# The residual of four layer norms: from a TensorE product with a scaled identity to a ScalarE write into the accumulator banks

## The chip, the cores and the metric

The kernel runs on one core of one Trainium2 chip. The metric is device time in microseconds (us) of one execution. Three runs of the kernel before took 918.62, 918.8 and 917.6 us; their median is 918.62 us.

## The reference

Two blocks follow each other on an activation `x` of 256 rows by 1024 columns. The first block has two sub-layers with an RMS norm after each (`x = x + rms_norm(m)`); nothing in it changes here. The second block has two layers, and each layer has a mixer and a feed-forward network (FFN), so four sub-layers:

```
ALPHA = (2.0 * DEPTH) ** 0.25
for layer in range(2):
    mix = concatenate([o_main, o_mem]) @ w_out      # layer 0: NSA attention, layer 1: MoBA attention
    x = layer_norm(ALPHA * x + mix, ln1_g[layer], ln1_b[layer])
    ffn = conv_ffn(x, ...)                          # up, convolution, gelu gate, down (2816 -> 1024)
    x = layer_norm(ALPHA * x + ffn, ln2_g[layer], ln2_b[layer])
```

The change touches how `ALPHA * x` gets into the sum with `mix` or `ffn`. Each of the four layer norms reads that sum from PSUM.

## The kernel before, in words

The 256 rows are two row blocks `q` of 128 rows. The output of a sub-layer for block `q` is 128 x 1024 and lies in two PSUM banks, `2q` and `2q+1` (index `z` is the half of 512 columns), so all four banks 0 to 3 hold the output of a sub-layer. Banks 4 and 5 take attention logits, 6 the transposed probabilities, 7 the attention outputs; in the FFN banks 4 to 7 take the up products.

Matrix products with weights are split: ScalarE (ACT) rounds a weight unit of 128 x 1024 from `raw` to `whi` (L622, called "split" or "hi" below), VectorE (DVE) computes the rest `wlo` (L628, "lo"), and TensorE (PE) adds three rounded products, activation high times weight high, low times high, high times low (L681, L684 and L687 in `pe_chunk`; L778 in `pe_project`, six instructions of 512 columns per unit and row block). The units arrive by DMA through four `raw` buffers and six split buffers.

The order of the work is written out by hand. `EVEN`, `ODD`, `NSA` and `MOBA` are lists of steps, `feed(l)` builds the list of FFN `l`. Each engine walks through the same list and does its own part of every step, strictly in that order. A step `("log", g)` is: PE computes logits (L858), DVE adds the mask and takes the minimum (L971), ACT takes the exponentials (L984). `("mul", g)` is DVE's normalisation, `("turn", g, side)` the transposes (L867) and a copy by ACT (side 0, L1031) or DVE (side 1, L1039), `("val", g)` the value product, `("fin", g)` the output's split, `("proj", s, n, q)` one unit of the output projection, and `("chunk"/"tile")` an input projection. With every step that uses a weight unit, ACT first splits units up to four ahead. `("cmp",)` is the logits of NSA's compressed keys (L1803 on PE, L1928 to L1933 on DVE, L1866 on ACT). `("T", k, q)` transposes a finished `x` (L716), ACT copies it as the high part `thi` (L723), DVE computes the low part `tlo` (L730). `("norm", ...)` is the layer norm: DVE's statistics (L1146), two passes into `rows` and `x` (L1152, L1160), and for `q` = 1 one weight "lo" (L628) between these two passes.

The residual is a step `("add_x", s, q)`, `pe_add_x`: two products of the matrix `scaled` (the identity times ALPHA, made by POOL at the start) with `x[:, q, half z]`, both in plain fp32, with `start=True` into banks `2q` and `2q+1`:

```
p.fill(2 * q + z, (*normed, q, z))
p.i.matmul(ps[:, 2 * q + z, :], scaled[:, :], x[:, q, half[z]], start=True, stop=False)
```

There are eight such steps: two in each of `NSA`, `feed(0)`, `MOBA`, `feed(1)`. In a mixer they stand in the middle of the list; banks 0 and 1 (NSA) or 0 to 2 (MoBA) were until then the banks that the input projections used in turn ("turn banks"). In an FFN `add_x 0` is the first step and `add_x 1` comes right after the transposes `T` of block 1. The projection `("proj", s, 0, q)` and the first `down` step accumulate onto what is there. `p.fill` waits until the bank's previous content has been read.

Of the kernel before, what the change touches and what calls it, by code (L numbers as in the profile page):

```python
# [263 lines left out]
def _build(nc, ctx, inp, out_dram, plan):  # L264
# [15 lines left out]
    tb = sb("tb", [P, 12 * T])  # L280
    stat = sb("stat", [P, 1024])
    ident = sb("ident", [P, P])
    scaled = sb("scaled", [P, P])
    tri = sb("tri", [P, T])
    relb = sb("relb", [32, 12])
    cols = sb("cols", [P, 4])
# [245 lines left out]
    for g in nsa[2:]:  # L532
# [9 lines left out]
        ("tile", "a_q", 2), ("log", n0), ("turn", m0, 0), ("turn", m0, 1), ("tile", "a_q", 3), ("mul", n0), ("turn", m1, 0),  # L542
        ("comp", 1), ("comp", 2), ("val", m0), ("turn", m1, 1), ("fin", m0), ("log", n1), ("tile", "a_q", 4), ("turn", n0, 0),
        ("turn", n0, 1), ("comp", 3), ("log", n2), ("tile", "a_q", 5), ("mul", n1), ("val", m1), ("mul", n2), ("fin", m1),
        ("turn", n1, 0), ("turn", n1, 1), ("log", n3), ("cmp",), ("add_x", "a", 0), ("turn", n2, 0), ("proj", "a", 0, 0),
        ("add_x", "a", 1), ("cmp2",), ("log", n4), ("cmpt", 0), ("turn", n2, 1), ("proj", "a", 1, 0), ("log", n5), ("mul", n3),
        ("proj", "a", 0, 1), ("val", n0), ("turn", n3, 0), ("mul", n4), ("proj", "a", 1, 1), ("fin", n0), ("turn", n3, 1), ("cmpt", 1),
        ("proj", "a", 2, 0), ("val", n1), ("fin", n1), ("turn", n4, 0), ("val", n2), ("fin", n2), ("log", n6), ("turn", n4, 1),
        ("proj", "a", 2, 1), ("mul", n5), ("val", n3), ("turn", n5, 0), ("fin", n3), ("log", n7), ("mul", n6), ("proj", "a", 3, 0),
# [19 lines left out]
        ("tile", "b_k", 3), ("turn", g2, 0), ("turn", g2, 1), ("tile", "b_q", 3), ("mul", g3), ("val", g2), ("fin", g2),  # L569
        ("turn", g3, 0), ("log", g4), ("turn", g3, 1), ("mul", g4), ("tile", "b_k", 4), ("chunk", "b_v1", 0, 0), ("val", g3),  # L570
        ("chunk", "b_v1", 0, 1), ("fin", g3), ("chunk", "b_v1", 1, 0), ("chunk", "b_v1", 1, 1), ("turn", g4, 0), ("tile", "b_q", 4),
        ("tile", "b_k", 5), ("tile", "b_q", 5), ("log", g5), ("add_x", "b", 0), ("proj", "b", 0, 0), ("log", g6), ("turn", g4, 1),
        ("mul", g5), ("proj", "b", 1, 0), ("add_x", "b", 1), ("proj", "b", 0, 1), ("turn", g5, 0), ("val", g4), ("proj", "b", 2, 0),
        ("mul", g6), ("turn", g5, 1), ("fin", g4), ("proj", "b", 1, 1), ("proj", "b", 2, 1), ("val", g5), ("fin", g5), ("turn", g6, 0),
        ("proj", "b", 3, 0), ("proj", "b", 4, 0), ("proj", "b", 5, 0), ("turn", g6, 1), ("proj", "b", 3, 1), ("val", g6),
        ("proj", "b", 6, 0), ("proj", "b", 7, 0), ("proj", "b", 4, 1), ("fin", g6), ("norm", "b", 0), ("proj", "b", 5, 1),
# [178 lines left out]
                          ).then_inc(*d.sig("mix_lo", s, i))  # L755


    def pe_project(p, s, n, q, residual):
        u = U[f"{s}_out"][n]
        if ("proj", s, n, q) in KEEP:  # L760
            p.fill(7)
            pe_keep(p, 7, "proj", s, n, q)
        wh, wl = weights(u)
        of, *step = ("out", gives[s, n, q].g) if (s, n, q) in gives else ("mix", s, n // 2)
        p.wait_ge("hi", u)
        p.wait_ge(of + "_hi", *step)
        hi, lo, k = mixed(n)
        xh, xl = hi[:, k, q * P:q * P + P], lo[:, k, q * P:q * P + P]
        passes = [(y, z) for y in range(3) for z in range(2)] if n < 7 else [(y, z) for z in range(2) for y in range(3)]
        for y, z in passes:  # L770
            x_, w_ = ((xh, wh), (xl, wh), (xh, wl))[y]
            if y == 1:
                p.wait_ge(of + "_lo", *step)
            if y == 2:
                p.wait_ge(*lo_of(u))
            if n == 0 and y == 0 and not residual:
                p.fill(2 * q + z, ("gained", POST[s], q, z))
            mm = p.i.matmul(ps[:, 2 * q + z, :], x_, w_[:, 0, 512 * z:512 * z + 512],  # L778
                            start=n == 0 and y == 0 and not residual, stop=n == 7 and y == 2)
            if n == 7 and y == 2:  # L780
                mm.then_inc(*p.sig("proj", s, q, z))
        if n < 7 and q:
            mm.then_inc(*p.sig("used", u))

    def pe_add_x(p, s, q, *normed):

        p.wait_ge("alpha", 0)
        for z in range(2):
            p.fill(2 * q + z, (*normed, q, z))
            p.i.matmul(ps[:, 2 * q + z, :], scaled[:, :], x[:, q, half[z]], start=True, stop=False)  # L790


    def scores(g, side, c):
# [507 lines left out]
    def pool_start(g):  # L1301
        g.i.memset(nhalf[:, :], -0.5).then_inc(*g.sig("nhalf", 0))
        g.i.memset(bl[:, 256:384], NEG).then_inc(*g.sig("bl_neg", 0))
        g.wait_ge("c_ident", "all")
        g.i.tensor_scalar(scaled[:, :], ident[:, :], ALPHA, None, ALU.mult).then_inc(*g.sig("alpha", 0))
        for what, *a in START:
            if what == "rms":
                pool_rms(g, "pre0", a[0])


    def pe_even(p):
        for what, *a in EVEN:
# [21 lines left out]
            elif what == "log":  # L1334
                pe_log(p, *a)
            elif what == "turn":
                pe_turn(p, *a)
            elif what == "val":
                pe_val(p, *a)
            elif what == "ret":  # L1340
                k = a[0]
                if 1 <= k <= 4:
                    h, slot = k - 1, sm[:, 4 + (k - 1) % 2, :]
                    c = slice(h * P, h * P + P)
                    if h == 0:
                        p.wait_ge("ev", "e_bv", 1)
                        p.fill(6, ("ret_out", 0))
                        p.fill(7, ("ret_out", 1))
                    pe_keep(p, 6, "ret", h, at=h * P)
                    p.wait_ge("decayed", h)  # L1350
                    p.i.matmul(ps[:, 6, c], slot[:, 0:128], E["bv"][:, 0, c], start=True, stop=True)
                    p.i.matmul(ps[:, 7, c], slot[:, 128:256], E["bv"][:, 0, c], start=True, stop=False)
                    p.i.matmul(ps[:, 7, c], slot[:, 256:384], E["bv"][:, 1, c], start=False, stop=True).then_inc(*p.sig("kept", h))
                if k in (0, 2):
                    p.wait_ge("rope", 3)
                    for z in range(2):
                        p.fill(4 + z, ("decayed", k + z))
                    for j, (c, i0, n) in enumerate(((0, 0, 256), (256, 128, 128))):
                        for y in range(2):
                            for z in range(2):  # L1360
                                o = 32 * (k + z)
                                mm = p.i.matmul(ps[:, 4 + z, c:c + n], E["post"][o:o + 32, 2 + y, j * P:j * P + P],
                                                E["post"][o:o + 32, y, i0:i0 + n], start=y == 0, stop=y == 1)
                                if j == y == 1:
                                    mm.then_inc(*p.sig("ret", k + z))
            elif what == "mix":
                for q in range(2):
                    p.wait_ge("gated", "b", q)
                pe_mix(p, *a)
            elif what == "proj":  # L1370
                pe_project(p, *a, False)
            elif what == "brow":
                p.wait_ge("c_bias", "relb")
                p.fill(3, ("brow", 0))
                p.i.matmul(ps[0:12, 3, 0:384], relb[:, :], hotrev, start=True, stop=True).then_inc(*p.sig("brow_t", 0))
# [160 lines left out]
    def pe_odd(p):  # L1536
        for what, *a in ODD:
# [53 lines left out]
            elif what == "mix":  # L1591
                for q in range(2):
                    p.wait_ge("gated", "c", q)
                pe_mix(p, *a)
            elif what == "proj":
                pe_project(p, *a, False)

    def act_odd(a):
        for what, *k in ODD:
# [161 lines left out]
    def pe_nsa(p):  # L1761
        for what, *a in NSA:
# [53 lines left out]
                pe_turn(p, *a)  # L1816
            elif what == "val":
                pe_val(p, *a)
            elif what == "add_x":
                pe_add_x(p, "a", a[1], "normed", "a")  # L1820
            elif what == "proj":
                pe_project(p, *a, True)

    def act_nsa(a):
        for what, *k in NSA:
# [50 lines left out]
                act_pt(a, *k)  # L1876
            elif what == "fin":
                act_out(a, "a", *k)

    def dve_nsa(d):  # L1880
        for what, *k in NSA:
# [93 lines left out]

    def feed(l):
        n, k = f"f_in{l}_0", (7, 10)[l]
        out = [("add_x", 0)] + by_rows(n, 0) + [("T", k, 1), ("add_x", 1)] + by_rows(n, 1)
        for j in range(1, 11):
            first = j == 1  # L1980
            out += [("up", j, 0)] + [("jt",)] * first + [("up", j, 1)] + [("conv", 0)] * first + [("up", j, 2)] + [("acts", 0)] * first
# [19 lines left out]
    def pe_ffn(p, l, before):  # L2001
        for what, *a in feed(l):
            if what == "T":
                pe_rows_t(p, *a)
            elif what == "add_x":
                pe_add_x(p, "f", a[0], "normed", f"f{l}")
            elif what == "chunk":
                pe_chunk(p, *a, ("up0", l, a[2]), 4 + a[2])
            elif what == "jt":
# [22 lines left out]
            elif what == "down":  # L2032
# [7 lines left out]
                final = j == 10 and z == 1  # L2040
                passes = [(y, n) for n in range(2) for y in range(3)] if final else [(y, n) for y in range(3) for n in range(2)]
                for y, n in passes:
                    g_, w_ = ((gh, wh), (gl, wh), (gh, wl))[y]
                    if y == 1:
                        p.wait_ge("glo", l, j)
                    if y == 2:
                        p.wait_ge(*lo_of(u))
                    mm = p.i.matmul(ps[:, 2 * q + n, :], g_, w_[:, 0, 512 * n:512 * n + 512], start=False, stop=final and y == 2)  # L2048
                    if final and y == 2:
                        mm.then_inc(*p.sig("down", l, q, n))  # L2050
                if not final and q == 1:
# [42 lines left out]
    def act_ffn(a, l, before, nxt):  # L2094
        for what, *k in feed(l):
# [3 lines left out]
            if what == "T":  # L2099
                act_rows_t(a, *k)  # L2100
                if k[1] == 1:
                    a.wait_ge("xw", before, 1, 1)
                    for i in nxt:
                        act_vec(a, i)
            elif what == "chunk" and k[1] == 3 and k[2] == 1:
                for q in range(2):
                    a.wait_ge("lin", k[0], q)
# [66 lines left out]
    def pe_moba(p):  # L2174
        for what, *a in MOBA:
# [9 lines left out]
                pe_turn(p, *a)  # L2185
            elif what == "val":
                pe_val(p, *a)
            elif what == "add_x":
                pe_add_x(p, "b", a[1], "normed", "b")
            elif what == "proj":  # L2190
                pe_project(p, *a, True)

    def act_moba(a):
        for what, *k in MOBA:
# [23 lines left out]
                act_pt(a, *k)  # L2218
            elif what == "fin":
                act_out(a, "b", *k)  # L2220

    def dve_moba(d):
        for what, *k in MOBA:
# [135 lines left out]
```

## Time and profile before

| what | value |
|---|---|
| median of three runs | 918.62 us (917.6 to 918.8) |
| profiled execution, span from first to last instruction | 918.4 us |
| mean granted TensorE clock | 0.996 of full speed |
| PE busy | 894.0 us, 97% |
| DVE busy | 650.5 us, 71% |
| ACT busy | 490.5 us, 53% |
| PE's share of the chain that ended last | 88% |
| the fp32 residual products (L790) | 32 instructions, 16.9 us busy |

The profiled execution's own time is not listed beside its span; the span is 0.2 us under the median of the runs, and times of the trace are set against that span. The chain that ended last is followed back from the last instruction, so a stretch of it that reads "PE" is one in which PE had work without waiting. A plain fp32 product appears as two instructions, so the 16 residual products are 32 rows of L790. Matmul records overlap each other, since the ends are modelled; the spacing of their starts, or a piece of the chain divided by its count, is what one costs.

### The profile page before, as it was taken

What the parts mean: (1) busy time and instruction counts of PE and PEld (TensorE: products, weight loads), DVE (VectorE), ACT (ScalarE), POOL (GpSimd) and SP (SyncE); (2) the same over time, 40 slices, a digit from 0 to 9 for tenths busy, and PEclk for the clock granted to TensorE, in tenths of its full rate; (3) what the DMA queues carried; (4) which work ended last, traced back from release to release, by engine and by line L of the source; (5) the groups of instructions that cost most, each with busy time, mean ns of one, the idle gap of its engine ahead of it and who ended that gap; (6) DMA issues with size and microseconds to landing.
All of it is one profiled execution on the core that took longest, in us unless ns stands there. A gap on an engine that the chain in (4) does not pass through costs nothing.

```text
span 918.4 us, 14567 instructions
## 1 busy us (share of the span) xinstructions
PE 894.0 (97%) x5692; PEld 770.2 (84%) x5692; DVE 650.5 (71%) x1182; ACT 490.5 (53%) x890; POOL 43.6 (5%) x73
## 2 busy tenths in 40 slices
PE   8999999899999999999999999999999999999997
PEld 8998988788977888677888888888997788888885
DVE  4769686755767657778786786786656778677676
ACT  5464474555775557553554455445655365454541
POOL 2005000200001100001000000000000100000000
PEclk9999999999999999999999999999999999999999
DMA  8845534374364652113566655645442456655561
GB/s 302 309 166 156 184 107 151 119 244 143 126 191 152 239 191 92 54 62 95 203 206 204 189 185 180 207 160 207 131 165 82 148 187 211 203 195 176 189 198 46
DMA packets 45504, 155.06 MB, mean 169 GB/s; under 512 B 5404, under 2 KB 8060, under 8 KB 45436
## 3 DMA queue, kind: packets, MB, share of 16 engines
q1 hardware_dynamic: 40688, 141.78, 46.1%
q10 hardware_dynamic: 4748, 12.36, 4.2%
q8 instruction: 45, 0.74, 0.3%
q14 instruction: 23, 0.19, 0.1%
HBM read 152.78 MB, written 1.34 MB: 168 GB/s over the span
## 4 chain that ended last, share of the span: by engine, by line
PE 88%; DVE 7%; ACT 3%; issue 1%; POOL 0%; DMA 0%; DVEq 0%; ACTq 0%
PE ps L2027 16%; PE ps L2048 13%; PE ps L778 8%; PE ps L2030 8%; PE ps L661 6%; PE ps L665 6%; PE ps L662 6%; PE ps L684 4%; PE ps L681 4%; PE ps L687 4%; PE ps L858 3%; PE ps L910 2%; PE ps L867 2%; PE ps L790 2%; DVE wlo L628 2%; PE ps L716 1%
## 5 line engine op out<-in xcount | busy, mean ns | idle before, releaser
L628 DVE TENSOR_TENSOR wlo<-raw,whi 128x1024 fp32r<-128x1024 f32 (+1 forms) x263 | 314.2, 1218 | 41.5 <-ACT whi L622 40.9
L622 ACT ACTIVATE whi<-raw 128x1024 fp32r<-128x1024 f32 (+1 forms) x263 | 271.5, 1047 | 98.1 <-DMA raw<-in_ws 37.4
L2027 PE MATMUL ps<-t,whi 128*128 128x512 f32 x640 | 160.0, 392 | 0.0
L2027 PEld LDWEIGHTS ps<-t,whi 128*128 128x128 f32 x640 | 116.2, 189 | 21.6
L661 PE MATMUL ps<-t,whi 128*128 128x256 f32 (+1 forms) x480 | 120.6, 289 | 0.3 <-ACT arena L1657 0.3
L662 PE MATMUL ps<-t,whi 128*128 128x256 f32 (+1 forms) x480 | 117.4, 283 | 0.0
L661 PEld LDWEIGHTS ps<-t,whi 128*128 128x128 f32 (+1 forms) x480 | 91.1, 190 | 5.6 <-issue 3.9
L2048 PE MATMUL ps<-whi,r 128*128 128x512 f32 x352 | 95.2, 390 | 0.0
L2030 PEld LDWEIGHTS ps<-t,wlo 128*128 128x128 f32 x640 | 87.3, 190 | 6.2
L662 PEld LDWEIGHTS ps<-t,whi 128*128 128x128 f32 (+1 forms) x480 | 91.3, 190 | 0.3
L2030 PE MATMUL ps<-t,wlo 128*128 128x256 f32 x640 | 89.2, 282 | 0.0
L2048 PEld LDWEIGHTS ps<-whi,r 128*128 128x128 f32 x352 | 64.9, 188 | 12.5
L665 PE MATMUL ps<-t,wlo 128*128 128x256 f32 (+1 forms) x480 | 67.3, 283 | 0.0
L665 PEld LDWEIGHTS ps<-t,wlo 128*128 128x128 f32 (+1 forms) x480 | 61.8, 191 | 0.0
L681 PE MATMUL ps<-whi,t 128*128 128x512 f32 (+3 forms) x208 | 57.2, 369 | 1.8 <-DVE arena L1690 1.5
L687 PE MATMUL ps<-wlo,t 128*128 128x512 f32 (+3 forms) x208 | 54.0, 353 | 1.8 <-DVE wlo L628 1.8
L984 ACT ACTIVATE sm<-sm,stat 128x128 f32<-128x128 f32 (+1 forms) x92 | 40.4, 441 | 27.3 <-DVE stat L971 27.1
L2048 PE MATMUL ps<-wlo,r 128*128 128x512 f32 x176 | 54.9, 390 | 0.0
L684 PE MATMUL ps<-whi,t 128*128 128x512 f32 (+3 forms) x208 | 54.4, 355 | 0.5 <-DVE t L730 0.5
L2146 DVE TENSOR_TENSOR r<-arena,r 128x512 fp32r<-128x512 f32 x22 | 15.2, 692 | 48.5 <-ACT r L2092 48.5
L2092 ACT ACTIVATE r<-arena 128x512 fp32r<-128x512 f32 x22 | 13.9, 633 | 62.8 <-PE ps L2048 58.4
L681 PEld LDWEIGHTS ps<-whi,t 128*128 128x128 f32 x208 | 34.2, 189 | 9.6 <-issue 4.3
(268 smaller groups left out, 1234.8 us busy)
## 6 DMA issues: line engine op xcount, KB each, us to landing
raw<-in_ws SPq DMA_DIRECT2D x256, 512.0 KB, 4.2
vecs<-in_vecs ACTq DMA_DIRECT2D x12, 512.0 KB, 6.2
arena<-in_ws ACTq DMA_DIRECT2D x5, 512.0 KB, 5.5
raw<-in_ws SPq DMA_DIRECT2D x4, 384.0 KB, 3.2
tb<-brow ACTq DMA_DIRECT2D x8, 192.0 KB, 5.2
rows<-in_mem SPq DMA_DIRECT2D x2, 512.0 KB, 4.0
x<-in_x SPq DMA_DIRECT2D x1, 1024.0 KB, 10.5
rows<-in_ws ACTq DMA_DIRECT2D x2, 512.0 KB, 4.3
```

What stands on the lines that cost most here:

```text
L622: a.i.activation(whi[:, j % NSPLIT, 0:n], raw[:, j % NRAW, 0:n], ACT.Copy).then_inc(*a.sig("hi", u))
L628: d.i.tensor_tensor(wlo[:, j % NSPLIT, 0:n], raw[:, j % NRAW, 0:n], whi[:, j % NSPLIT, 0:n].bitcast(F), ALU.subtract).then_inc(*d.sig("lo" ...
L661: p.i.matmul(ps[0:m, b, 0:T], wh[:, k, :], thi[:, k, :], start=k == 0, stop=False)
L662: p.i.matmul(ps[0:m, b, 0:T], wh[:, k, :], tlo[:, k, :], start=False, stop=False)
L665: mm = p.i.matmul(ps[0:m, b, 0:T], wl[:, k, :], thi[:, k, :], start=False, stop=k == 7)
L681: p.i.matmul(ps[:, b, 0:n], thi[:, k0 + kl, q * P:q * P + P], wh[:, kl, :], start=k == 0 and kl == 0, stop=False)
L684: p.i.matmul(ps[:, b, 0:n], tlo[:, k0 + kl, q * P:q * P + P], wh[:, kl, :], start=False, stop=False)
L687: mm = p.i.matmul(ps[:, b, 0:n], thi[:, k0 + kl, q * P:q * P + P], wl[:, kl, :], start=False, stop=final and kl == nk - 1)
L778: mm = p.i.matmul(ps[:, 2 * q + z, :], x_, w_[:, 0, 512 * z:512 * z + 512], start=n == 0 and y == 0 and not residual, stop=n == 7 and y == 2)
L2027: p.i.matmul(ps[:, b, :], wh[:, k, :], t2[:, k, :], start=k == 0, stop=False)
L2030: mm = p.i.matmul(ps[:, b, 0:T], wl[:, k, :], thi[:, k, :], start=False, stop=k == 7)
L2048: mm = p.i.matmul(ps[:, 2 * q + n, :], g_, w_[:, 0, 512 * n:512 * n + 512], start=False, stop=final and y == 2)
```

## The change

`scaled` and POOL's instruction that made it are gone. The step `add_x` becomes `seed_x`:

- ACT writes `ALPHA * x[:, q, half z]` into bank `2q+z` with a Copy activation of 128 x 512 and signals `seeded` (`act_seed_x`, two instructions per step, 16 in all). The first product of the projection, or of the first `down` step, waits for `seeded` and accumulates.
- In the two mixers PE first runs one rounded product with `start=True` into each of the four banks (`pe_open`: `thi[:, 0, 0:P]` times `t2[:, 0, :]`, 512 columns), which signals `opened`; ACT waits for that before it overwrites the bank. In the FFNs, where the same banks were output banks before, there is no such product, PE does nothing in this step and ACT waits for `x` (`xw`).
- The lists move a little. In `NSA` the second step now stands before `("proj", "a", 0, 0)` instead of behind it. In `MOBA` `("log", g6)` now stands between the first `seed_x` and `("proj", "b", 0, 0)`. In `feed` the steps stand where they stood.

```diff
-        ("turn", n1, 0), ("turn", n1, 1), ("log", n3), ("cmp",), ("add_x", "a", 0), ("turn", n2, 0), ("proj", "a", 0, 0),
-        ("add_x", "a", 1), ("cmp2",), ("log", n4), ...
+        ("turn", n1, 0), ("turn", n1, 1), ("log", n3), ("cmp",), ("seed_x", "a", 0), ("turn", n2, 0), ("seed_x", "a", 1), ("proj", "a", 0, 0),
+        ("cmp2",), ("log", n4), ...
...
-        ("tile", "b_k", 5), ("tile", "b_q", 5), ("log", g5), ("add_x", "b", 0), ("proj", "b", 0, 0), ("log", g6), ("turn", g4, 1),
-        ("mul", g5), ("proj", "b", 1, 0), ("add_x", "b", 1), ("proj", "b", 0, 1), ("turn", g5, 0), ("val", g4), ("proj", "b", 2, 0),
+        ("tile", "b_k", 5), ("tile", "b_q", 5), ("log", g5), ("seed_x", "b", 0), ("log", g6), ("proj", "b", 0, 0), ("turn", g4, 1),
+        ("mul", g5), ("proj", "b", 1, 0), ("seed_x", "b", 1), ("proj", "b", 0, 1), ("turn", g5, 0), ("val", g4), ("proj", "b", 2, 0),
...
-            if n == 0 and y == 0 and not residual:
+            if n == 0 and y == 0 and s in POST:
                 p.fill(2 * q + z, ("gained", POST[s], q, z))
+            if n == 0 and y == 0 and s not in POST:
+                p.wait_ge("seeded", s, q, z)
...
-    def pe_add_x(p, s, q, *normed):
-        p.wait_ge("alpha", 0)
+    def pe_open(p, s, q):
         for z in range(2):
-            p.fill(2 * q + z, (*normed, q, z))
-            p.i.matmul(ps[:, 2 * q + z, :], scaled[:, :], x[:, q, half[z]], start=True, stop=False)
+            p.fill(2 * q + z, ("normed", s, q, z))
+            p.i.matmul(ps[:, 2 * q + z, :], thi[:, 0, 0:P], t2[:, 0, :], start=True, stop=True).then_inc(*p.sig("opened", s, q, z))
+
+    def act_seed_x(a, s, q, *free):
+        for z in range(2):
+            a.wait_ge(*free, q, z)
+            a.i.activation(ps[:, 2 * q + z, :], x[:, q, half[z]], ACT.Copy, scale=ALPHA).then_inc(*a.sig("seeded", s, q, z))
...
-        out = [("add_x", 0)] + by_rows(n, 0) + [("T", k, 1), ("add_x", 1)] + by_rows(n, 1)
+        out = [("seed_x", 0)] + by_rows(n, 0) + [("T", k, 1), ("seed_x", 1)] + by_rows(n, 1)
...
+                    if j == z == y == 0:
+                        p.wait_ge("seeded", f"f{l}", q, n)
...
+            elif what == "seed_x":
+                act_seed_x(a, f"f{l}", *k, "xw", before)
```

## Rows read from the trace of the kernel before

**Rows 1.** The page: span, busy time by engine, chain by engine
```profile
span 918.4 us, 14567 instructions
PE 894.0 (97%) x5692; PEld 770.2 (84%) x5692; DVE 650.5 (71%) x1182; ACT 490.5 (53%) x890; POOL 43.6 (5%) x73
...
PE 88%; DVE 7%; ACT 3%; issue 1%; POOL 0%; DMA 0%; DVEq 0%; ACTq 0%
```

**Rows 2.** Groups by shape: busy us, mean ns | idle before
```profile
L790 PE MATMUL ps<-x,scaled 128*128 128x512 f32 x32 | 16.9, 654 | 0.0
...
L723 ACT ACTIVATE t<-ps 128x512 fp32r<-128x512 f32 x28 | 15.4, 596 | 28.0 <-PE ps L716 27.9
...
L2085 ACT ACTIVATE arena<-arena 128x512 f32<-128x512 f32 x22 | 13.8, 625 | 1.3 <-DVE arena L2128 1.3
```

**Rows 3.** Chain in time, NSA's middle: start us, us, what
```profile
369.23 3.47 PE ps L790 x4
...
373.17 1.39 PE ps L778 x6
374.55 1.72 PE ps L790 x4
376.27 1.06 PE ps L858 x8
```

**Rows 4.** Windows: busy by engine, then granted clock, DMA
```profile
370.00:372.00 2.00, 2.00 (x4) 0.83 (x3) 1.93 (x4) 1.99 (x10) 0.00 (x0) 0.50 0.00 0
```

**Rows 5.** Timeline of ACT, NSA's middle: start us, us, instruction
```profile
371.50 0.49 ACT L1866 ACTIVATE arena<-arena 128x360 f32<-128x360 f32 x1
...
373.70 1.05 ACT L622 ACTIVATE whi<-raw 128x1024 fp32r<-128x1024 f32 x1
```

**Rows 6.** Chain in time, MoBA's middle
```profile
690.89 1.91 PE ps L790 x4
692.80 1.39 PE ps L778 x6
694.19 1.06 PE ps L858 x8
695.25 0.59 PE ps L867 x4
695.84 1.39 PE ps L778 x6
...
698.94 1.38 PE ps L778 x6
```

**Rows 7.** Timeline of DVE and ACT, MoBA's middle
```profile
692.62 0.08 DVE L971 DVE_READ_ACCUMULATOR2_ANT stat<- 128x1 f32 x1
...
692.74 0.40 ACT L984 ACTIVATE sm<-sm,stat 128x128 f32<-128x128 f32 x1 [3.16 <-DVE stat L971]
...
695.84 1.04 ACT L622 ACTIVATE whi<-raw 128x1024 fp32r<-128x1024 f32 x1
696.80 0.51 ACT L984 ACTIVATE sm<-sm,stat 128x256 f32<-128x256 f32 x1
...
698.78 1.05 ACT L622 ACTIVATE whi<-raw 128x1024 fp32r<-128x1024 f32 x1
```

**Rows 8.** Timeline of DVE, then chain: start of the first FFN
```profile
432.15 1.41 DVE L1160 SCALAR_TENSOR_TENSOR x<-rows,stat,vecs 128x512 f32<-128x512 f32 x2
...
433.48 1.22 DVE L628 TENSOR_TENSOR wlo<-raw,whi 128x1024 fp32r<-128x1024 f32 x1
...
436.90 0.47 PE ps L684 x2
```

**Rows 9.** Timeline of DVE, then chain: start of the second FFN
```profile
729.67 1.41 DVE L1160 SCALAR_TENSOR_TENSOR x<-rows,stat,vecs 128x512 f32<-128x512 f32 x2
...
731.00 1.22 DVE L628 TENSOR_TENSOR wlo<-raw,whi 128x1024 fp32r<-128x1024 f32 x1
...
734.73 0.46 PE ps L684 x2
```

More of the change, by code:

```diff
@@ L282, in _build @@
     ident = sb("ident", [P, P])
-    scaled = sb("scaled", [P, P])
     tri = sb("tri", [P, T])
@@ L544, in _build @@
         ("turn", n0, 1), ("comp", 3), ("log", n2), ("tile", "a_q", 5), ("mul", n1), ("val", m1), ("mul", n2), ("fin", m1),
-        ("turn", n1, 0), ("turn", n1, 1), ("log", n3), ("cmp",), ("add_x", "a", 0), ("turn", n2, 0), ("proj", "a", 0, 0),
-        ("add_x", "a", 1), ("cmp2",), ("log", n4), ("cmpt", 0), ("turn", n2, 1), ("proj", "a", 1, 0), ("log", n5), ("mul", n3),
+        ("turn", n1, 0), ("turn", n1, 1), ("log", n3), ("cmp",), ("seed_x", "a", 0), ("turn", n2, 0), ("seed_x", "a", 1), ("proj", "a", 0, 0),
+        ("cmp2",), ("log", n4), ("cmpt", 0), ("turn", n2, 1), ("proj", "a", 1, 0), ("log", n5), ("mul", n3),
         ("proj", "a", 0, 1), ("val", n0), ("turn", n3, 0), ("mul", n4), ("proj", "a", 1, 1), ("fin", n0), ("turn", n3, 1), ("cmpt", 1),
@@ L755, in dve_mix, with pe_project @@
                           ).then_inc(*d.sig("mix_lo", s, i))
-    def pe_project(p, s, n, q, residual):
+    def pe_project(p, s, n, q):
         u = U[f"{s}_out"][n]
@@ L775, in pe_project @@
                 p.wait_ge(*lo_of(u))
-            if n == 0 and y == 0 and not residual:
+            if n == 0 and y == 0 and s in POST:
                 p.fill(2 * q + z, ("gained", POST[s], q, z))
-            mm = p.i.matmul(ps[:, 2 * q + z, :], x_, w_[:, 0, 512 * z:512 * z + 512],
-                            start=n == 0 and y == 0 and not residual, stop=n == 7 and y == 2)
+            if n == 0 and y == 0 and s not in POST:
+                p.wait_ge("seeded", s, q, z)
+            mm = p.i.matmul(ps[:, 2 * q + z, :], x_, w_[:, 0, 512 * z:512 * z + 512], start=n == 0 and y == 0 and s in POST,
+                            stop=n == 7 and y == 2, skip_group_check=s not in POST)
             if n == 7 and y == 2:
@@ L1303, in pool_start @@
         g.i.memset(bl[:, 256:384], NEG).then_inc(*g.sig("bl_neg", 0))
-        g.wait_ge("c_ident", "all")
-        g.i.tensor_scalar(scaled[:, :], ident[:, :], ALPHA, None, ALU.mult).then_inc(*g.sig("alpha", 0))
         for what, *a in START:
@@ L1370, in pe_even @@
             elif what == "proj":
-                pe_project(p, *a, False)
+                pe_project(p, *a)
             elif what == "brow":
@@ L1595, in pe_odd @@
             elif what == "proj":
-                pe_project(p, *a, False)
+                pe_project(p, *a)
     def act_odd(a):
@@ L1818, in pe_nsa @@
                 pe_val(p, *a)
-            elif what == "add_x":
-                pe_add_x(p, "a", a[1], "normed", "a")
+            elif what == "seed_x":
+                pe_open(p, *a)
             elif what == "proj":
-                pe_project(p, *a, True)
+                pe_project(p, *a)
     def act_nsa(a):
@@ L1878, in act_nsa @@
                 act_out(a, "a", *k)
+            elif what == "seed_x":
+                act_seed_x(a, *k, "opened", k[0])
     def dve_nsa(d):
@@ L2004, in pe_ffn @@
                 pe_rows_t(p, *a)
-            elif what == "add_x":
-                pe_add_x(p, "f", a[0], "normed", f"f{l}")
             elif what == "chunk":
@@ L2042, in pe_ffn @@
                 for y, n in passes:
+                    if j == z == y == 0:
+                        p.wait_ge("seeded", f"f{l}", q, n)
+                        p.fill(2 * q + n, ("normed", f"f{l}", q, n))
                     g_, w_ = ((gh, wh), (gl, wh), (gh, wl))[y]
@@ L2047, in pe_ffn @@
                         p.wait_ge(*lo_of(u))
-                    mm = p.i.matmul(ps[:, 2 * q + n, :], g_, w_[:, 0, 512 * n:512 * n + 512], start=False, stop=final and y == 2)
+                    mm = p.i.matmul(ps[:, 2 * q + n, :], g_, w_[:, 0, 512 * n:512 * n + 512], start=False, stop=final and y == 2, skip_group_check=True)
                     if final and y == 2:
@@ L2104, in act_ffn @@
                         act_vec(a, i)
+            elif what == "seed_x":
+                act_seed_x(a, f"f{l}", *k, "xw", before)
             elif what == "chunk" and k[1] == 3 and k[2] == 1:
@@ L2187, in pe_moba @@
                 pe_val(p, *a)
-            elif what == "add_x":
-                pe_add_x(p, "b", a[1], "normed", "b")
+            elif what == "seed_x":
+                pe_open(p, *a)
             elif what == "proj":
-                pe_project(p, *a, True)
+                pe_project(p, *a)
     def act_moba(a):
@@ L2220, in act_moba @@
                 act_out(a, "b", *k)
+            elif what == "seed_x":
+                act_seed_x(a, *k, "opened", k[0])
     def dve_moba(d):
```

## The prediction

> **What bounds the kernel now.** I read the page first, then the chain in order of time around the eight residual steps, then the timeline of each engine there, and last the granted clock. The page says that PE is the bound: it is busy for 97% of a span of 918.4 us and makes up 88% of the chain that ended last, while ACT is at 53% [rows 1]. So instructions taken from PE are worth their spacing, and ACT has time on average. But an average says nothing of the moment at which a seed is needed, and both engines walk through the same list in order. So each of the four places is worked out by its own clock.
>
> The residual products are 32 instructions, 16.9 us busy [rows 2]. In the chain a step of four instructions lasts 1.72 us (so 0.86 us per product) at six of the eight places, of which [rows 3] and [rows 6] show how it looks, 1.91 us at the first MoBA step and 3.47 us at the first NSA step. In all 15.7 us. The 3.47 us has a reason: from 370 to 372 us the granted clock is 0.50, that is 1.2 instead of 2.4 GHz [rows 4]; just before stand 24 tiny products of the compressed keys (L1803, 32 columns each). A rounded product of 512 columns is spaced 0.232 us (six in 1.39 us, [rows 3]).
>
> **Bounds of the whole.** If everything on ACT were hidden, PE would save 15.7 us less eight opening products of 0.23 us (1.9 us), so 13.8 us. This is the far end. Now the places.
>
> **A seed's price on ACT.** The trace has no ACT write from SBUF into PSUM. Its nearest rows are 128 x 512 from PSUM (0.60 us) and within SBUF (0.63 us) [rows 2]; I take 0.60 us to its end and 0.50 us from start to start (ACT's instructions overlap by about 0.1 us, as the split of 1.04 us at 695.84 followed by a start at 696.80 shows [rows 7]). Bounds: 0.4 and 0.7 us. From its end to PE's start I take 0.1 us (an estimate; ACT starts 0.04 us after DVE's last row there, [rows 7]).
>
> **A, NSA's middle.** On ACT the seeds stand behind `log n3` and `cmp`. ACT is in the middle of these exponentials until 371.99 us, where the exponential of the compressed logits (L1866) ends [rows 5]; DVE's mask work sets that, not PE, so it stays. Seeds 0 then end at about 372.5 and 373.0. PE, after the compressed logits at 369.23, runs two opening products, the turn of n2 and two more opening products; even at half clock that is 4 x 0.43 + 0.9 = 2.6 us, done at 371.8. It then waits. `proj a 0 0` starts its first product at 372.6, its second at 373.1, and five more spacings end it at 374.3. Before, the next step (`log n4`, L858) began at 376.27 [rows 3]. Gain 2.0 us. Seeds 1 come behind n2's copy, end by 374.6, and are needed only after `proj a 1 0`, later. The split at 373.70 [rows 5] slips by some 0.9 us, into time in which ACT waited for the next logits. So of 5.2 us of products only 2.0 come back, since PE arrives early and waits. Were the clock in the kernel before not to fall there, its step would be 1.7 us shorter and A worth only 0.3 us.
>
> **C, MoBA's middle.** Here the list hurts. On ACT `seed_x b 0` stands behind `log g5`, whose eight exponentials start at 692.74, released by DVE's mask that ended at 692.70, and end when the split starts at 695.84 [rows 7]. So seeds 0 run from 695.84 to 696.44 and to 696.94. PE ends the logits of g5 at 690.89 as before [rows 6], opens two banks until 691.35, and then meets `log g6`, which needs banks 4 and 5 from that same mask: it waits until 692.8 and ends at 693.9. Then `proj b 0 0`, with everything behind it, waits for ACT: first product 696.5, second 697.0, end 698.2. Before, the same steps (residual, projection, log g6) were over at 695.25 [rows 6]. Loss 2.9 us. The turn (0.59) and `proj b 1 0` (1.39) bring PE to 700.2, two opening products to 700.6. ACT meanwhile: exponentials of g6 from 696.8 (1.98 us, 696.80 to 698.78 in [rows 7]) to 698.8, two splits (1.9 us) to 700.7, then seeds 1, ended at 701.3 and 701.8. `proj b 0 1` ends at 703.1. Before it ended at 700.32 [rows 6]. So C costs 2.8 us in all, although two steps (3.6 us) were taken from PE. Behind it the chain is PE's own until the norm, so nothing gives this back. Bounds: with seeds of 0.4 us it costs 2.4, with 0.7 us 3.1.
>
> **B and D, the heads of the FFNs.** Nothing is opened and nobody waits for these seeds before the first `down`, many us later. ACT's two seeds (1.1 us) stand before a split with idle time behind it. The first removed step (1.72 us) lets block 0's chunks run early. But then comes `T` of block 1, which needs x from DVE (L1160): its halves are ready at 432.9 and 433.6 in B, 730.4 and 731.1 in D [rows 8, 9], and DVE was busy throughout before that with other work, so this doesn't move. PE ends its chunks at about 432.7 (B) and 730.3 (D), held a little by the last "lo" of that weight, and waits. The transposes end by 434.1 and 731.6. With the second step gone PE wants `tlo`, and DVE first has its weight split of 1.22 us, until 434.70 (B) and 732.22 (D) [rows 8, 9], then 0.7 us for `tlo`. So L684 starts at about 435.5 instead of 436.90, and 732.95 instead of 734.73 [rows 8, 9]: gains 1.4 and 1.8 us, of 3.44 each. From there to the norm PE is never short of splits, and the gain stays. Bounds: 0 (all of it turned into waits on DVE) and 3.4 us each.
>
> **Rest.** POOL's instruction at the start (the identity times ALPHA) and the waits on it cost nothing either way: POOL is busy for 5% [rows 1]. No DMA is moved; loads of `raw` follow the splits, which slip by at most 3 us in C, with PE behind by as much.
>
> **The sum.** -2.0 (A) - 1.4 (B) + 2.8 (C) - 1.8 (D) = -2.4 us on 918.4 us, so a span of 916.0. The median of the runs is 0.2 us above the span, so 916.2 us.
>
> **The clock, and a page against it.** The one fall in the trace came after products with few columns and cost the residual step 1.75 us (3.47 against 1.72, [rows 3, 4]). In C the change makes PE wait twice, 1.4 and 2.6 us, with 1.1 us of half-height logits between. If the clock falls there to 1.2 GHz for as long, PE's work behind 696.5 takes twice its time, at most 1.7 us more, of which 0.9 us disappear in the wait for seeds 1: 0.8 us left. The same at A behind 372.6 has no such cover: 1.7 us. The Trainium skill ("TensorE: Matmul & The Clock Gate", Part 1) says that the default is the half rate, that a stretch of little activity on TensorE brings it back and a busy stretch lifts it. By that rule C falls; the trace has a fall at A, and no gap like C's.
>
> **Rivals.**
> 1. The clock falls on dense work in both mixers, at A and at C: 918.4 - 2.4 + 0.8 + 1.7 = 918.5 span, or with no cover in C 919.4; with the 0.2 that is 918.7 to 919.6, and I take 919.1. It decides from 2.4 us of added half-clock work on; beyond that the change is slower. For it: the gaps that C gets. Against it: dense products before and after.
> 2. The heads of the FFNs give nothing: the removed products become waits for DVE's `x` and `tlo`. 918.4 - 2.0 + 2.8 = 919.2, so 919.4 with the 0.2, slower. For it: DVE has no gap there; against: 1.22 us of that row is over early enough by my count.
> 3. C is hidden after all (seeds reach ACT before the exponentials, or later slack swallows the wait): C gives 0 to -3.2, the time is 913.4 to 910. For it only ACT's 53%; against: the order of the list.
> 4. All of it hidden: 13.8 us, 904.8. Against: A, B, C and D each show the wait that comes next.
> 5. A fall only at C: 917.0.
>
> **Chances.** Forecast 0.46; fall only at C (5) 0.20; rival 1 0.09; rival 2 0.08; rival 3 0.14; rival 4 0.03. Under 0.2% (1.8 us) a measurement of this kernel can't be told from no change. The forecast's own spread of about 1.3 us straddles that bound (916.8): about two thirds of it count as faster; with rivals 3 and 4, 0.49. Within 0.2%: the rest of the forecast, most of (5), half of 1: 0.37. Slower: 0.14. The range, 912.8 to 919.4, takes in the bounds of seeds and of the FFN heads and part of rival 3.
>
> **What would show it.** In the changed trace: no L790; the four seeds of MoBA and NSA as ACT rows of about 0.6 us. At C PE idle for about 2.6 us with the seed as releaser, and again about 0.9 us; if that is missing, C is wrong. At A one wait of about 1 us for the seed. At the head of each FFN waits for L1160 and L730 on PE. In the FFN bodies nothing changes. The forecast is wrong if PE's idle time grows by less than 3 us or if a half-clock stretch appears over dense products.

## The result: 0.2% slower

The kernel after takes 920.24 us (median of 13 runs, 918.62 to 921.59), the kernel before on the same chip 918.74 us (13 runs, 917.08 to 919.8). The ratio is 1.0019, 95% interval 1.0011 to 1.0027. The forecast was 916.2 us and "faster"; the time also lies above the range.

Page of the kernel after, to be set against [rows 1]:

```profile
span 917.1 us, 14544 instructions
PE 885.4 (97%) x5668; PEld 765.2 (83%) x5668; DVE 650.4 (71%) x1182; ACT 498.2 (54%) x906; POOL 42.9 (5%) x72
...
PE 84%; DVE 10%; ACT 4%; issue 1%; POOL 0%; DMA 0%; ACTq 0%; DVEq 0%
```

The work moved as written: PE lost 8.6 us of busy time (894.0 to 885.4), ACT gained 7.7 us (490.5 to 498.2). But in the chain PE went from 88% to 84% and DVE and ACT rose by as much. Products left PE, and PE waited in their place.

The span misleads. It is 1.3 us shorter than that of [rows 1], while the median is 1.5 us longer. Every further execution has its own time listed beside its span, and the time is 1.8 or 1.9 us more each time: this one took 918.9 us with a span of 917.1. So the execution of before that I had as a trace (span 918.4) took about 920.2 us (worked out, its own time isn't listed), 1.5 us over that kernel's median. The execution of after that was profiled is the second fastest of its 13. So one profile lies above its kernel's median and the other below its own, and the two spans differ in the wrong direction.

To find the places I cut each span at the same instructions: a, the start of DVE's scaling of n2 in `arena`, ahead of NSA's middle; b, the first transpose of the compressed weights; c, the first `up` product of the first FFN; d, the copy of the last q tile ahead of MoBA's middle; e, the first product of `turn g5 0`; f, the first `up` product of the second FFN. All lengths are in us, worked out from the timelines:

```
                      0-a    a-b(A) b-c(B)   c-d   d-e(C) e-f(D)  f-g    span
before (rows 1)      362.84  14.42  64.50  247.44  10.96  39.40  178.84  918.4
before again (e5)    362.58  12.73  64.48  247.42  10.97  39.40  178.82  916.4
after                362.12  12.60  63.24  247.44  15.03  37.84  178.83  917.1
after again (e1)     362.10  14.16  63.20  247.42  16.20  37.86  179.16  920.1
```

The bodies c-d and f-g stay within 0.02 us, but for 0.3 us in f-g of e1. The stretch ahead of a is the same code in all four, and what it varies by is no effect of the change. Against the second execution of before the four places give -0.13, -1.24, +4.06 and -1.56: together +1.1 us in one execution of after, and +3.8 in another (+1.43, -1.28, +5.23, -1.54). The medians, 1.5 us apart here and 3.6 us in a later comparison, lie within these.

**NSA's middle, A.** Chain of the kernel after in order of time (start us, us, what); L779 is its projection and L864 its logits, L778 and L858 in [rows 3]:

```profile
367.68 3.19 ACT sm L990 x16
370.87 0.39 ACT arena L1870
371.26 0.49 ACT ps L796
...
371.89 1.83 PE ps L779 x6
373.72 1.06 PE ps L864 x8
```

ACT's eight exponentials (x16, since each is followed by a short read of its sum), the compressed one and the first seed (L796) stand in a row, then PE starts six products. They take 1.83 us and not the 1.39 us of [rows 3], at full clock: the second of them waits for the second seed. No residual step of 1.72 us stands between projection and logits any more, but PE has waited for the seed instead, 1.93 us in its timeline. That is the exchange I drew, and it gives 0.1 us. The wait brings no fall of the clock here. The window (its length; busy time of PE, PEld, DVE, ACT, POOL; then granted clock, DMA share, GB/s):

```profile
370.00:372.00 2.00, 0.11 (x1) 0.14 (x1) 2.00 (x4) 2.00 (x9) 0.00 (x0) 1.00 0.00 0
```

**MoBA's middle, C**, the same view; here the chain of [rows 6] was PE alone:

```profile
688.94 3.19 ACT sm L990 x16
692.13 0.49 ACT ps L796
...
692.75 2.93 PE ps L779 x6
695.69 0.65 PE ps L873 x4
696.34 1.38 PE ps L779 x6
697.71 0.24 PE ps L790
...
697.98 0.61 ACT ps L796
...
698.63 0.50 PE ps L779
...
699.15 1.44 PE ps L779 x5
```

Six products took 2.93 us at 692.75 and 1.38 us at 696.34. The second number is that of [rows 3]. The first is to be set against the 1.83 us that A shows for six products right behind a seed at full clock: 1.1 us more. The waits of PE in 686 to 703 us (line waited for: us in total, times, longest):

```profile
PE ps L779 <- ACT ps L796: 3.1, 2, 2.7
PE ps L864 <- DVE stat L977: 1.2, 1, 1.2
```

And the windows of two us, in the same columns:

```profile
690.00:692.00 2.00, 0.10 (x2) 0.00 (x0) 1.86 (x9) 2.00 (x12) 0.00 (x0) 1.00 0.00 0
692.00:694.00 2.00, 1.25 (x3) 1.01 (x4) 0.74 (x1) 2.00 (x8) 0.00 (x0) 0.65 0.10 27
694.00:696.00 2.00, 2.00 (x7) 1.51 (x7) 0.00 (x0) 2.00 (x8) 0.00 (x0) 0.50 0.61 236
696.00:698.00 2.00, 2.00 (x11) 1.49 (x9) 1.52 (x4) 1.05 (x3) 0.00 (x0) 1.00 0.00 0
```

PE stands nearly idle from 690 to 692 us, at a granted clock of 1.00. A mean of 0.65 from 692 to 694 us, 0.50 behind it and 1.00 from 696 on put the fall to 0.50 (1.2 of 2.4 GHz) at 692.6 to 696.0 us: it begins at the end of the gap, just before the products start at 692.75, and covers all of them. So the gap costs once as a wait and once more as slow work after it. The Trainium skill ("TensorE: Matmul & The Clock Gate", Part 1) says that little activity on TensorE brings the half rate back. The trace agrees at C; at A a wait of 1.93 us brought no fall.

**The heads of the FFNs, B and D.** Chain of the kernel after at the start of the first and then of the second FFN, beside [rows 8, 9]:

```profile
432.14 0.61 DVE t L729
...
432.80 0.74 PE ps L683 x2
```

```profile
730.02 1.32 DVE x L1166 x2
731.35 1.14 DVE wlo L627
732.48 0.61 DVE t L729
...
733.14 0.73 PE ps L683 x2
```

PE is released by DVE's `t`, which stands behind `x` and the weight split, as forecast. The starts of L683 here and L684 in [rows 8, 9] can't be compared by the clock time, since what lies ahead differs; the segments B and D can.

**The seed's price.** 16 seeds in the group by shape, 589 ns each; I had taken 600 and bounded it by 400 and 700:

```profile
L796 ACT ACTIVATE ps<-x 128x512 f32<-128x512 f32 x16 | 8.9, 589 | 1.8 <-PE ps L790 0.9 <-issue 0.9
```

### The profile page after: what moved, and what is told of

Read it like the earlier page. It is cut to its first block, busy times and chain, and to the rows that moved or that the text cites. A ratio compares the mean times of both kernels' runs of the same rounds, so it can differ in the third digit from the quotient of the medians.

```text
span 917.1 us, 14544 instructions
## 1 busy us (share of the span) xinstructions
PE 885.4 (97%) x5668; PEld 765.2 (83%) x5668; DVE 650.4 (71%) x1182; ACT 498.2 (54%) x906; POOL 42.9 (5%) x72
## 4 chain that ended last, share of the span: by engine, by line
PE 84%; DVE 10%; ACT 4%; issue 1%; POOL 0%; DMA 0%; ACTq 0%; DVEq 0%
PE ps L2031 16%; PE ps L2055 13%; PE ps L779 8%; PE ps L2034 8%; PE ps L660 6%; PE ps L664 6%; PE ps L661 6%; PE ps L683 3%; PE ps L686 3%; PE ps L680 3%; PE ps L864 3%; DVE wlo L627 3%; PE ps L916 2%; PE ps L873 2%; DVE sm L977 1%
## 5 line engine op out<-in xcount | busy, mean ns | idle before, releaser
L683 PE MATMUL ps<-whi,t 128*128 128x512 f32 (+3 forms) x208 | 54.6, 356 | 1.2 <-DVE t L729 1.2
L686 PEld LDWEIGHTS ps<-wlo,t 128*128 128x128 f32 x208 | 35.3, 189 | 9.3 <-DVE wlo L627 4.2
```

The costliest lines, as they stand in the source:

```text
L683: p.i.matmul(ps[:, b, 0:n], tlo[:, k0 + kl, q * P:q * P + P], wh[:, kl, :], start=False, stop=False)
L686: mm = p.i.matmul(ps[:, b, 0:n], thi[:, k0 + kl, q * P:q * P + P], wl[:, kl, :], start=False, stop=final and kl == nk - 1)
```

## The experiments

Two theories stood: that C's waits on ACT cost about 3 us by themselves and the fall of the clock that they bring adds to it, while the FFN heads earn their part; and, as rival, that the clock did nothing lasting and the FFN heads' gain was lost to DVE. Four kernels ran beside the kernel before on one chip (before: 918.6 us, 31 runs), four more on another (918.73 us, 23 runs).

**e1, the kernel after once more.** No edit.

> The changed kernel once more, for a second trace. Theory: the changed kernel's place C (MoBA's middle) has the clock at 1.2 GHz for a few us in nearly every execution, so this trace shows a half-clock stretch near 693 us again (about +1.3 us there beside the waits) and in the slower executions further ones; time 1 to 2 us above the kernel before. Rival (the falls are rare and the 1.5 us come from somewhere else, such as ScalarE's writes slowing TensorE): half-clock stretches are no more frequent than before, and the places A, B, D differ from the first trace.

Measured: 922.17 us (11 runs, 918.73 to 923.39), ratio 1.0031 [1.002, 1.0043], so 3.6 us slower by the medians, more than I had expected. The profiled execution has long falls, from 368.9 to 375.7 and from 693.2 to 700.0 us (worked out from windows as above). Chain in C:

```profile
694.24 2.93 PE ps L779 x6
697.17 0.85 PE ps L873 x4
698.02 2.34 PE ps L779 x6
```

Now the second projection is slow too (2.34 against 1.38 us). Over all 24 executions of after none has a mean granted clock above 0.997, 21 have 0.996 or less and 14 have 0.994 or less. Of 54 executions of before in the two batches 37 have 0.998 or more, 11 have 0.997 and six 0.996, the lowest. The profiled execution of after, with one short fall, has 0.997, this one with two long ones 0.992, and one of before without any (e5, below) 0.999. The other traced executions with one short fall have 0.996 or 0.997 too. So the kernel after has a fall nearly always, and in the 18 of 24 executions with 0.995 or less more than one short one; that is read from the means, the falls themselves are seen in the traced executions alone.

**e2, PE kept at work in the waits.** The kernel after, plus small products into a bank that nobody reads:

```
+WARM = {("a", 0): 6, "log": 5, ("b", 0): 11, ("b", 1): 0}
 def pe_project(p, s, n, q):
...
+    if n == 0 and y == z == 0 and (s, q) in WARM:    # ahead of the wait for the seed
+        p.fill(7)
+        for _ in range(WARM[s, q]):
+            p.i.matmul(ps[:, 7, 0:P], ident[:, :], ident[:, :], start=True, stop=True)
...                                                   # the same 5 times ahead of log g6
```

> The changed kernel with small identity products (128 columns, plain fp32) put into TensorE's three waits of the mixers: 6 in front of NSA's first projection, 5 in front of the logits of MoBA's last group, 11 in front of MoBA's first projection. They fill waits and add no work that is needed. Theory (the clock): the waits stay as long as they were, the half-clock stretches at A and C go, and the time falls by 1 to 2.5 us against the changed kernel, to between 0 and 1 us under the kernel before. Rival (no part of the loss is the clock's): the time stays at the changed kernel's or rises a little, by the products that overrun the waits (under 0.5 us).

Measured: 919.47 us (11 runs, 916.89 to 921.38), ratio 1.0003 [0.9992, 1.0013], so 2.7 us under e1 of the same batch (a little more than I had expected) and 0.9 us above before. Segment C is 13.95 us and shows no fall to 0.50; its products behind the second seeds take 1.42 us for five, against 1.43 or 1.44 elsewhere at full clock, although they wait for the same seeds:

```profile
693.88 1.00 ACT ps L801 x2
694.88 2.01 ACT sm L999 x8
696.89 1.90 ACT whi L622 x2
...
699.84 1.42 PE ps L784 x5
```

```profile
696.00:698.00 2.00, 2.00 (x12) 1.68 (x11) 1.05 (x3) 2.00 (x6) 0.00 (x0) 0.95 0.61 225
```

The chain runs over ACT here: seeds 0, the four exponentials of g6, the two splits, then seeds 1, one after another. The granted clock of this one execution reads 0.95 and not 1.00 up to 710 us, which the last section takes up; the other ten have means of 0.996 to 0.999, and none of them the 0.995 or less of 18 of the 24 executions of after. So without a fall to half, C costs 3.0 us (13.95 against 10.97), which is the waits alone; the fall adds 1.1 us where it is short and 2.2 us where it is long.

**e3, the FFN part alone.** In both mixers the scaled product by PE and the old order of the list; in the FFNs the seed by ACT:

```
+BY_PE = ("a", "b")
 def pe_open(p, s, q):
+    if s in BY_PE: ... p.i.matmul(ps[:, 2*q+z, :], scaled[:, :], x[:, q, half[z]], start=True, stop=False) ... return
```

> The change in the two FFNs alone; both mixers as in the kernel before (identity products, order of the list). Theory (the change gains in the FFNs and loses in the mixers): 2.5 to 3.2 us faster than the kernel before (B 1.3 and D 1.6 us in the first trace of the changed kernel). Rival (the FFN heads' gain is given back later, or ScalarE's writes cost there): within 1 us of the kernel before.

Measured: 916.42 us (8 runs, 915.81 to 918.42), ratio 0.9974 [0.9964, 0.9984], 2.2 us faster by the medians, just under the 2.5 to 3.2 us that I had expected. B is 63.21 and D 37.83 us: -1.27 and -1.57 against e5. The heads of the FFNs are worth 2.8 us. In this execution some went again: the body c-d is 248.14 instead of 247.42 us, and its chain has a row that neither before nor after has:

```profile
435.68 6.94 DMA raw<-in_ws
...
443.61 0.59 ACT arena L2087
```

A load of a raw weight unit became the last thing to arrive. That PE comes nearer to those loads the earlier it is would fit, but it isn't shown: the kernel after has the same B without such a row.

**e4, both mixers' seeds earlier.** NSA's ahead of `log n3`, MoBA's ahead of `log g5`, so that no exponentials stand before a seed on ACT:

```
-("log", g5), ("seed_x", "b", 0), ("log", g6), ("proj", "b", 0, 0), ... ("seed_x", "b", 1)
+("seed_x", "b", 0), ("seed_x", "b", 1), ("log", g5), ("proj", "b", 0, 0), ("log", g6), ...
-("log", n3), ("cmp",), ("seed_x", "a", 0), ("turn", n2, 0), ("seed_x", "a", 1), ...
+("seed_x", "a", 0), ("seed_x", "a", 1), ("log", n3), ("cmp",), ("turn", n2, 0), ...
...
+moba[-3].turn_banks, ... = (6,), ...      # g4's second transposes use bank 6 alone
```

> The change with the seeds of both mixers moved ahead: both NSA seeds and their opening products in front of the logits of n3, both MoBA seeds in front of the logits of g5, where ScalarE is idle for about 3 us; the projection stands before log g6 again, and group g4's second transposes use bank 6 alone instead of 6 and 3. Theory (the loss at A and C is the place of the seed behind exponentials in ScalarE's order): TensorE waits for no seed, the mixers gain their products less the opening ones, 3.4 - 0.9 = 2.5 us each (3.6 - 0.9 at C), and with the FFNs' 2.9 us the kernel is 7 to 8.5 us faster than before, about 911. Rival (a seeded bank or ScalarE's share is the cost, wherever it stands): less than 4 us faster.

Measured: 917.43 us (11 runs, ten of them 915.37 to 918.67), 1.2 us faster by the medians, ratio 0.9981 [0.9971, 0.999]. C is 9.02 us, 1.95 less than before. But A is 13.80, longer than both in e5 (12.73) and in the kernel after (12.60). PE waits 1.05 us for DVE's work on the compressed keys:

```profile
376.50 0.55 PE L1815 MATMUL ps<-ident,arena 128*128 128x128 f32 x3 [1.05 <-DVE arena L1959]
```

The chain shows why that work is late:

```profile
365.94 0.61 DVE pt L1045
...
366.59 0.50 PE ps L790
...
368.19 2.81 PE ps L1807 x24
...
371.09 0.29 DVE arena L1934
```

The opening products (L790) now stand ahead of `log n3`, and the last of them waits until DVE has read its bank (L1045). So `log n3`, the compressed logits (L1807) and DVE's first row on them (L1934) come late, the last of these 8.39 us behind a, against 6.49 us in e5 and in the kernel after. From there the chain is DVE's up to PE's row at 376.50. There is a fall too (from 371.1 to 374.5 us), but the half-clock products are not in the chain: PE waits behind them. So at A the price is that of the place of the opening products. My expectation for this kernel, about 911 us, was missed by 6 us: I had again summed up what PE saves. The rival's number (less than 4 us faster) came out, but not by its cause, since C gained with the same seeds on ACT.

**e5, the kernel before once more.** No edit.

> The kernel before once more, for a second trace. Theory: the fall of the clock in NSA's middle, which the first trace shows, is rare in this kernel (its faster executions have a mean granted clock of 0.998 or 0.999, that trace 0.996). So this trace most likely has no half-clock stretch there, the piece from DVE's scaling of n2 to the first transpose of the compressed weights lasts about 12.7 us instead of 14.4, and the changed kernel's 12.6 us there is no gain. Rival (the fall belongs to this kernel and A is a real gain): 14.4 us again.

Measured: 918.26 us (10 runs, 917.28 to 919.8), ratio 0.9997 [0.9988, 1.0006]; profiled execution 918.22 us, span 916.4. Its chain at A and its window, beside [rows 3, 4]:

```profile
368.97 1.80 PE ps L790 x4
...
372.59 1.72 PE ps L790 x4
```

```profile
370.00:372.00 2.00, 2.00 (x11) 1.35 (x10) 1.97 (x4) 2.00 (x10) 0.00 (x0) 1.00 0.00 0
```

The first residual step takes 1.80 us and not 3.47, at a granted clock of 1.00. Every other segment agrees to 0.02 us, apart from the start. So the fall at A comes in some executions only. Five traces have NSA as in the kernel before: three show no fall there and 12.72 or 12.73 us for A (e5, e7, e8), two show one, the first trace (14.42 us) and e3, with 14.40 us. Its first residual step (L794 there):

```profile
367.85 2.92 PE ps L794 x4
```

By the means, 37 of the 54 executions of before have 0.998 or more, above every traced execution with a fall (0.997 or less). So an execution without it is the usual one.

**e6, NSA's part alone**, and **e7, MoBA's part alone**: as e3, with `BY_PE = ("b", "f0", "f1")` and `("a", "f0", "f1")`.

> The change in NSA alone; MoBA and both FFNs as before. Theory: no gain without a fall of the clock and a loss of 1 to 1.7 us in the executions with one behind the wait: 0 to 1.5 us slower than before. Rival (the forecast's A): 2 us faster.

> The change in MoBA alone, with its order of the list; NSA and both FFNs as before. Theory: 4.1 us slower (2.8 us of waits for the seeds behind ScalarE's exponentials and 1.3 us of half clock), 4 to 5.2 us with longer falls. Rival (waits only, no clock): 2.8 us slower.

Measured: e6 919.03 us (12 runs), ratio 1.0005 [0.9994, 1.0016]; e7 923.26 us (5 runs), ratio 1.005 [1.0038, 1.0062], 4.5 us slower. In e6 segment A is 12.61 us. It has a fall of its own (from 367.5 to 370.9 us), but over ACT's exponentials, where PE waits anyway. PE's six products behind it take 1.85 us, as in the kernel after without a fall at A (1.83 us), so this fall costs nothing:

```profile
366.73 3.19 ACT sm L1000 x16
...
370.94 1.85 PE ps L781 x6
```

In e7 C is 15.34 us, against 10.97. The chain shows the fall (from 695.2 to 698.6 us) over the end of one projection, a turn and most of the next projection:

```profile
694.01 2.34 PE ps L781 x6
696.35 0.85 PE ps L883 x4
697.20 2.08 PE ps L781 x6
```

```profile
696.00:698.00 2.00, 2.00 (x8) 1.67 (x7) 0.69 (x2) 2.00 (x4) 0.00 (x0) 0.50 0.40 160
```

The parts add up: -0.26% (e3), +0.05% (e6) and +0.50% (e7) make +0.29%, between the two measurements of the whole, +0.19% and +0.31%.

**e8, what the runs point to.** The FFN part by ACT, MoBA's seeds early as in e4, NSA as before (`BY_PE = ("a",)`).

> A version meant to beat both kernels: the FFNs as in the changed kernel, MoBA's seeds ahead of the logits of g5 (as in the run with early seeds, g4's second transposes in bank 6), NSA as in the kernel before. Theory: -1.3 (B) - 1.6 (D) - 1.9 (C, where DVE's mask and scaling then set the pace: 9.0 us instead of 11.0 in the run with early seeds) = -4.8 us against the kernel before, about 913.8, since without NSA's change there is no idle TensorE there and no frequent fall. Rival (the run with early seeds gained little because of C, not because of NSA): about 917, no better than the run with early seeds.

Measured: 915.6 us (5 runs, 913.79 to 915.75), ratio 0.9963 [0.9951, 0.9975]: faster than both kernels, by 3.1 us against before by the medians, where I had expected 4.8. Chain in C:

```profile
693.02 0.42 DVE sm L987
...
694.48 0.60 DVE pt L1055
...
695.28 1.31 DVE sm L1018 x2
...
696.72 0.63 PE ps L883 x4
```

No seed and no half-clock product stands in it. C is 9.03 us, so 1.94 of the 3.6 us of removed products come back; DVE's mask and scaling of g6 is late next. B and D keep -1.31 and -1.54. These are 4.8 us in all, of which the body c-d takes back 0.96 us behind a late load of raw weights (7.19 us in its chain at 435.94), and f-g 0.40 us, with another such load in its chain (6.66 us at 731.20).

## Why the prediction was wrong

Two terms of the sum failed, and each has a reason of its own. The forecast's own sign of being wrong came true as well: half-clock stretches over dense products.

**Term A, -2.0 us, measured -0.13.** It was worked out against a residual step at half clock (3.47 us), which e5 shows to be no part of the usual execution. The case set beside it, that without that fall A is worth only 0.3 us, was the right one. The mechanism at A (PE early, then waiting for a seed behind ACT's exponentials) was right. What let the trace pass as a typical one was the step "the median of the runs is 0.2 us above the span". About 1.8 us lie outside the span, so that execution was itself some 1.5 us over the median. I had three runs without a span of their own and took the nearness of 918.4 and 918.62 for a match. The 0.2 us did no harm to the base, which was again the median of the runs; it did harm through A, with 1.9 us.

**Term C, +2.8 us, measured +4.1 and +5.2**, was right as to the waits and wrong as to what they bring. The waits are there by place and size: 1.2 us for DVE's mask (1.4 forecast), 2.7 us for the seed (2.6), and 3.0 us in total without a fall (e2). The first product of `proj b 0 0` starts 7.35 us behind landmark d; the forecast's 696.5 is 7.30 us behind. But the sum put the clock at nothing, and the fall to 1.2 GHz at C was left to two rivals with chances of 0.20 and 0.09, when both traced executions of after have it, e7's too. And its price was put at 0.8 us, since 0.9 us should vanish in the wait for seeds 1. It was 1.1 us where the fall lasted 3.4 us, and 2.2 us where it lasted 6.8 us.

**B -1.4 and D -1.8** were right: -1.24 and -1.56, with DVE's `t` last, as said. Rival 2, that they give nothing, is refuted by e3. **The seed's price** (0.60 us, measured 0.589) and the opening product (0.23 us, measured 0.24) were right. Rival 3 is refuted as the kernel stands, but e8 shows that at C the order of the list stands in its way: its C is 1.94 us under before. (Its bound of -3.2 us was too far by the forecast's own numbers: 3.6 us less four opening products of 0.23 us is 2.7.) Rivals 1 and 5 have the mechanism: a fall at C alone is the first trace of after, falls at both mixers are e1. In e1 A's price is the forecast one (1.6 us, where it gave 1.7) and C's is nearly three times the forecast one (2.2 us, where it gave 0.8). The number nearest to the result, the 919.4 us of rival 2, is luck, since its cause is the refuted one.

With A at -0.1, C at +4.1 to +5.2 and B and D as measured, the sum becomes +1.1 to +2.3 us on the median of before, 918.74, so 919.9 to 921.0; measured 920.24. The 922.17 of e1 lies above that, and its trace has a long fall at A as well, worth 1.6 us there (14.16 against 12.60).

**Open.** Why the fall is short in some executions and long in others. Why late loads of raw weights come in the kernels with the FFN part, and how often. The chains of e2, e3, e4 and e8 have one or two of them in c-d (0.7 to 2.0 us in all), those of e1, e4 and e8 one in f-g; the first trace of after has none, and neither have the four traces with the FFNs as before (before, e5, e6, e7). No run moved those loads.

## What to carry to other kernels

Work given to a less busy engine is ready when that engine's own order comes to it: look up what stands ahead of it there, here eight exponentials that wait for a third engine, before its average load is counted. Where a move lets TensorE stand idle next to light work, price the gap and the half-clock products behind it, since the second was here a third to three quarters of the first. An instruction that only opens a bank takes a place in the order as well: in e4 one waited for a read of its bank and held up the logits behind it. And before a sum is made against a trace, ask whether that execution is typical: its own time against the median, and each stretch below full clock against a second execution.

## What the hardware showed that I had not expected

- An execution's time is 1.8 to 1.9 us above its span, in every one of the 140 runs that list both.
- A mean granted clock under 1 need not slow anything. The profiled execution of e2 has 0.95 from about 7 to about 710 us and then 1.00, mean 0.959. Yet its C has five products of 512 columns in 1.42 us (1.44 in the kernel after), and its whole span is 918.2 us, where 5% of 704 us would be 35 us. What this level stands for no run shows.
- One execution of e4 took 1238.12 us at a mean granted clock of 0.655; the ten others took 915.37 to 918.67 us at 0.995 to 0.998. No trace of it was taken, and the cause stays open.
- A fall that lies over a wait costs nothing: in e6 the clock is at half for 3.4 us and A is as long as without (12.61 and 12.60 us). The same length behind the wait costs 1.1 us at C in the kernel after.
- A write by ACT of 128 x 512 from SBUF into PSUM takes 589 ns, beside 596 from PSUM and 625 within SBUF in [rows 2].
